# Gated linear attention between the projection chunks, and the output projection in two halves

## The reference

```python
sh1, sc1, gt1, sh2, sc2, gt2 = split(silu(c) @ w_ada + b_ada, 6)        # adaLN, w_ada 1024 x 6144
h = rms_norm(x, g_mix) * (1 + sc1) + sh1
gq, gk, gv, gg, glr, fq, fk, fv, ff = split(h @ w_in)                   # w_in 1024 x 3096
# GLA: 4 heads, key 64, value 128, blocks of 64 tokens (the sample has one block of 32)
log_a = log_sigmoid(glr @ w_gk2 + b_gk) / 16
o_gla = gla_chunked(gq, gk, gv, log_a, s0)     # scores in a block, states from block to block
o_gla = rms_norm(o_gla, g_gla) * silu(gg)
# FoX: 8 heads of 64, softmax(q k / 8 + cumulated log forget), the sample also over 512 cached rows
o_fox = rms_norm(fox_attention(fq, fk, fv, logf), g_fox)
x = x + gt1 * (concat(o_gla, o_fox) @ w_out)                            # the output projection
h = rms_norm(x, g_ffn) * (1 + sc2) + sh2
x = x + gt2 * (routed_experts(h, top 8 of 64) + shared_expert(h))       # gate, up: 1024 x 256, down: 256 x 1024
y = rms_norm(x, g_final)
```

## Time and profile before

| | |
|---|---|
| time, median of 3 runs | 796.29 us (795.01 to 797.1) |
| time of the profiled execution | 796.61 us |
| its span, first to last instruction | 794.9 us |
| mean granted TensorE clock | 0.951 |
| PE busy / VectorE / ScalarE / GpSimd | 743.5 / 358.7 / 227.0 / 49.6 us |
| moved by DMA | 254.51 MB, mean 320 GB/s |

### The profile page before, as it was taken

The page is one execution under the profiler, slowest core; times in us unless marked ns, Lnnn a source line. Parts: engine busy times, 40 slices in busy tenths (PEclk is TensorE's granted clock), DMA queues, the critical chain, the costliest instruction groups (busy, mean ns, idle before and its releaser), DMA issues.

```text
span 794.9 us, 15663 instructions
## 1 busy us (share of the span) xinstructions
PE 743.5 (94%) x4903; PEld 462.9 (58%) x4903; DVE 358.7 (45%) x955; ACT 227.0 (29%) x423; POOL 49.6 (6%) x217
## 2 busy tenths in 40 slices
PE   6599999779898898999999899999999999999994
PEld 3299997564688575544455455456444555445553
DVE  1464434643512573444444344344543445434456
ACT  2453335405511332222222122222222222222223
POOL 4000002320002100000000000000000000000033
PEclk9789998978789899999999999999999999999998
DMA  9965353927485423999999999999997899999951
GB/s 353 381 202 206 115 210 114 415 78 251 174 338 231 171 107 117 384 392 381 426 425 426 425 425 426 425 427 425 426 425 292 360 425 426 423 425 427 425 242 60
DMA packets 47183, 254.51 MB, mean 320 GB/s; under 512 B 9344, under 2 KB 9680, under 8 KB 19072
## 3 DMA queue, kind: packets, MB, share of 16 engines
q1 hardware_dynamic: 43616, 248.70, 77.1%
q10 hardware_dynamic: 2752, 3.32, 1.3%
q0 software_dynamic: 736, 1.52, 0.5%
HBM read 250.86 MB, written 2.67 MB: 319 GB/s over the span
## 4 chain that ended last, share of the span: by engine, by line
PE 85%; DMA 7%; DVE 5%; ACT 2%; issue 1%; SPq 0%; DVEq 0%; ACTq 0%
PE psum L1247 23%; PE psum L1283 11%; PE psum L941 9%; PE psum L1214 8%; DMA expert_w<-in_w_exp_up 5%; PE psum L1134 4%; PE psum L1228 4%; PE psum L1229 3%; PE psum L1221 3%; PE psum L1162 2%; PE psum L908 2%; DMA pair<-in_w_in 1%; PE psum L1152 1%; PE psum L1269 1%; PE psum L894 1%
## 5 line engine op out<-in xcount | busy, mean ns | idle before, releaser
L1247 PE MATMUL psum<-expert_w,xg 128*32 128x512 f32 (+1 forms) x1312 | 199.6, 596 | 4.9 <-DMA expert_w<-in_w_exp_up 3.4
L1247 PEld LDWEIGHTS psum<-expert_w,xg 128*32 128x32 f32 (+1 forms) x1312 | 60.5, 120 | 140.6 <-issue 139.0
L1713 DVE TENSOR_TENSOR acc<-psum,acc 128x288 f32<-128x288 f32 x224 | 97.0, 454 | 66.2 <-PE psum L1229 65.0
L1283 PE MATMUL psum<-expert_w,hidT 128*32 128x512 f32 (+1 forms) x656 | 102.1, 596 | 0.0
L1727 DVE TENSOR_TENSOR hid<-psum,silg 128x256 f32<-128x256 f32 x28 | 11.9, 425 | 143.9 <-ACT silg L717 143.9
L1214 PE MATMUL psum<-h2hl,sel 128*128 128x512 f32 x290 | 76.3, 393 | 0.5 <-ACT acc L699 0.5
L1228 PE MATMUL psum<-comb,yhi 128*128 128x288 f32 x224 | 74.3, 340 | 0.0
L1229 PE MATMUL psum<-comb,ylo 128*128 128x288 f32 x224 | 64.5, 295 | 0.0
L1283 PEld LDWEIGHTS psum<-expert_w,hidT 128*32 128x32 f32 (+1 forms) x656 | 28.1, 119 | 53.7 <-issue 53.7
L717 ACT ACTIVATE silg<-psum 128x256 f32<-128x256 f32 x28 | 10.7, 384 | 169.4 <-PE psum L1247 169.4
L1228 PEld LDWEIGHTS psum<-comb,yhi 128*128 128x128 f32 x224 | 42.5, 190 | 25.4 <-issue 23.1
(11 more groups left out here) (351 smaller groups left out, 931.5 us busy)
## 6 DMA issues: line engine op xcount, KB each, us to landing
expert_w<-in_w_exp_down SPq DMA_DIRECT2D x64, 1024.0 KB, 18.9
expert_w<-in_w_exp_gate SPq DMA_DIRECT2D x64, 1024.0 KB, 19.2
expert_w<-in_w_exp_up SPq DMA_DIRECT2D x64, 1024.0 KB, 19.8
ring<-in_w_ada SPq DMA_DIRECT2D x24, 1024.0 KB, 7.1
pair<-in_w_in SPq DMA_DIRECT2D x6, 2048.0 KB, 10.3
pair<-in_w_out SPq DMA_DIRECT2D x2, 2048.0 KB, 10.3
x_tok<-in_x_prompt SPq DMA_DIRECT2D x2, 512.0 KB, 4.4
cacheK<-in_cache_fox_k ACTq DMA_DIRECT2D x1, 1024.0 KB, 5.6
```

Of the source, the lines that this page charges most:

```text
L1247: last = mm(bank[3][at:at + w, :].rearrange("p (g n) -> p g n", g=2), xg[:, k, at:at + w], expert_w[:, q:q + 2, DE * k:DE * k + DE], start ...
L1283: last = mm(bank[4 + half][at:at + w, :], hidT[:, i, at:at + w], expert_w[:, slot_of(g, DOWN, x), o:o + 512], start=i == 0, stop=i == 1, t ...
L1713: dve.tensor_tensor(acc[:, k, :], bank[6 + k % 2][:, 0:N], acc[:, k, :], ALU.add).then_inc(s["acc_ok"], 1)
```

## The change

It moves work in the part ahead of the expert blocks, and leaves the code of the second norm, the router and the expert blocks as it is.

- **Start.** x's transposes, the sum of squares and `ada(0, 0..2)` are mixed on PE. Two of the four copies of `ada_rows(0)` go to VectorE, and three of the eight prompt parts of `hhi` (`HHI_DVE`). The first projection piece is loaded as two halves with counters of their own. Chunks 0 and 1 take their passes in turns (both high by high, both low by high, both high by low).
- **Projection.** Chunks rotate over banks 0 to 2 and no more over 0 to 3. Banks 4 to 7 hold what now stands between the chunks: narrow projections after chunk 3, gates after 5, transposes of the GLA values after 9, cumulated forget values after 11 and 13, `ada(1, k)` after 15, 17, 21 and 22, GLA scores after 18, state updates after 20, GLA outputs of the prompt after 22. VectorE and ScalarE take their parts in the same way, between a copy and the next `wlo` or `whi`.
- **Output gate.** silu(gg) is taken in one ScalarE instruction where it lies, features on partitions, and is multiplied in when the transposed output is copied out (`gated`). Its 12 transposes to tokens go. `o_tok` becomes `o_gla` and `o_fox`.
- **FoX.** The first two units start right after chunk 23; the GLA output of the sample, transposes of FoX values and keys, and those of the cached keys stand between their steps. The FoX key and value copies are shared by VectorE and ScalarE. The norm of o_gla and the transposes of it (`mixed_T(0..3)`) come in units 4 to 7, and `ada_T(2)` in the last.
- **Output projection.** `mix(k, range(4))` (the GLA half) for k = 0 to 3 before the FoX output is ready, then four transposes of `o_fox`, then the rest.

The core of the diff on PE:

```diff
         pe.wait_ge(s["sc_ok"], 1)
         for k in range(KC):
+            if k >= 4:
+                pe.wait_ge(s["xT_ok"], k - 3)
+            for i in range(3):
+                last = tr(bank[k % 4][:, T0[i]:T0[i] + TN[i]], x_tok[0:TN[i], i, k::KC], ident[0:TN[i], 0:TN[i]])
+            last.then_inc(s["xT_ps"], 1)
+            if k in (3, 6):
+                ada(0, k // 3 - 1, 5)
...
+        for c in range(24):
+            if c >= 3:
+                pe.wait_ge(s["z_act" if (c - 3) % 2 else "z_dve"], (c - 3) // 2 + 1)
+            if c >= 2:
+                z_pass(c, whi, hhi)
+                z_pass(c, wlo, hhi)
+            z_pass(c, whi, hlo).then_inc(s["z_ps"], 1)
+            if c == 3:
+                narrow()
+            if c == 5:
+                gates()
+            if c == 9:
+                gla_values()
+            if c == 11:
+                cumulate()
+            if c == 13:
+                cumulate_past()
+            if c in (15, 17):
+                ada(1, c - 15, 3)
+                ada(1, c - 14, 3)
+            if c == 18:
+                gla_scores()
+            if c == 20:
+                gla_updates()
...
+                gla_out(range(4))
...
+        for p in (2, 3):
+            pe.wait_ge(s["exp_ok"], LAST + p - 2)
+            mixed_T(p, o_gla, P * p)
         values(LAST)
...
+        pe.wait_ge(s["mT_dve"], 4)
+        for k in range(4):
+            if k == 3:
+                pe.wait_ge(s["ada_ok"], 3)
+            mix(k, range(4))
         pe.wait_ge(s["po_ok"], 3)
...
+        pe.wait_ge(s["fox_ok"], 3)
+        for p in range(4, KC):
+            mixed_T(p, o_fox, P * (p - 4))
```

and on ScalarE in the last units of FoX:

```diff
+            if u == 4:
+                act.wait_ge(s["ssq_act"], 12)
+                act.activation(rs5[:, :, 0:4], ssq5[:, :, 0:4], ACT.Sqrt, bias=epst[:, 0:1], scale=1.0 / GV).then_inc(s["rs_act"], 1)
             if u == 6:
+                ada_rows(2, 3)
                 act.wait_ge(s["po_ok"], 2)
```

More of the change, by code:

```diff
@@ L300, in layer, with hhi_of_act @@
     FIRST_KEY = (N + 1) * E
+    HHI_DVE = (1, 3, 5)
+    def hhi_of_act(k):
+        return len([x for x in range(k + 1) if x not in HHI_DVE])
     GATE, UP, DOWN = range(3)
@@ L631, in _ @@
[L631 to L634 removed]
+        ada_rows(1, 3)
         act.wait_ge(s["zeros"], 2)
@@ L923, in _ @@
         for k in range(KC):
+            if k >= 4:
[5 more added lines that the diff above has]
+                ada(0, k // 3 - 1, 5)
+        for k in range(KC):
+            pe.wait_ge(s["sq_ok"], k + 1)
+            last = mm(bank[6][:, 0:N], ones[:, :], sq[:, k, :], start=k == 0, stop=k == KC - 1)
+            if k == 3:
+                ada(0, 2, 5)
@@ L1011, in blocks, with cumulate_past @@
+        def cumulate_past():
+            pe.wait_ge(s["state_in"], 48)
+            pe.wait_ge(s["tok_dve"], 3)
+            for j in range(4):
+                for t in range(j, 4):
+                    last = mm(bank[4][0:FH, P * j:P * j + P], pastf[:, t, :], (lower if t == j else ones)[:, :],
+                              start=t == j, stop=t == 3)
+            last.then_inc(s["crow_ps"], 1)
+        def blocks(some):
+            for b in some:
                 i, pb, n = b // 2, 64 * (b % 2), BLK if b < 4 else NS_
@@ new lines, in z_pass @@
+        def z_pass(c, w, h):
+            g, q = c // 2, c % 2
+            pe.wait_ge(s["whi_ok" if w is whi else "wlo_ok"], g + 1)
+            for k in range(KC):
+                if c == 0 and h is hhi and w is whi:
+                    pe.wait_ge(s["hhi_act"], hhi_of_act(k))
+                    pe.wait_ge(s["hhi_dve"], k + 1)
+                if c == 0 and h is hlo:
+                    pe.wait_ge(s["hlo_ok"], k + 1)
+                last = mm(bank[c % 3][:, 0:N], w[g % 2][:, k, P * q:P * q + P], h[:, k, :],
+                          start=k == 0 and w is whi and h is hhi, stop=k == KC - 1 and h is hlo)
+            return last
@@ new lines, in mixed_T @@
+        def mixed_T(p, o, at):
+            for i in range(3):
+                last = tr(bank[MIX_BANK[p]][:, T0[i]:T0[i] + TN[i]], o[0:TN[i], i, at:at + P], ident[0:TN[i], 0:TN[i]])
+            last.then_inc(s["mT_ps"], 1)
+        scores(0)
+        scores(1)
+        pe.wait_ge(s["z_act"], 12)
+        pe.wait_ge(s["z_dve"], 12)
+        gla_out((4,))
+        for i in range(3):
+            if i == 2:
+                pe.wait_ge(s["go_ok"], 3)
+            tokens(i, FV0, TOK_BANK[i])
+        ada_T(1, 1)
@@ L1103, in _ @@
+        ada(2, 3, 3)
+        values(1)
+        scores(2)
+        for u in range(2, LAST + 1):
             if u < LAST:
                 scores(u + 1)
-            if u < 2:
-                ada(2, 2 * u, 3)
-                ada(2, 2 * u + 1, 3)
-            elif u < 6:
+            if u < 6:
                 ada(2, u + 2, 3)
+            if u == 6:
+                pe.wait_ge(s["gla_ok"], 3)
+                pe.wait_ge(s["po_ok"], 2)
+                mixed_T(0, o_gla, 0)
+            if u == LAST:
+                pe.wait_ge(s["mT_dve"], 1)
+                mixed_T(1, o_gla, P)
+                ada_T(2, 3)
```

718 lines of the change are left out of this document (402 added, 316 removed).

## The result

The changed kernel takes 784.12 us (median; 783.97 to 787.31) where the kernel before takes 796.69 in the same comparison. The ratio is 0.9852, 95% interval 0.9828 to 0.9877. It is faster, but by 12.6 us and not by the 29.7 that the sum gave, and it lies outside the range of 757 to 781. The profiled execution took 783.97 us (span 782.2, mean granted clock 0.965).

What follows compares the result with a forecast made beforehand. PE was taken as the bound: expert blocks unchanged, and a 254.7 us chain ahead with waits and half-rate work. Its terms summed to 225.0, 29.7 us sooner, so 796.6 became 767 us; range 757 to 781, its own 759 to 776.

Steps and rivals of the forecast that it cites:

- Chunks 2 to 23, 70.5: Projection chunks on PE: 70.5 us as before, with the three-bank rotation costing nothing.
- the rival by which it becomes the bound: Projection: VectorE's added steps make each `wlo` late, PE waits every 6.4 us, 800 us at 3.0 a pair; chance 0.04.
- Between the chunks, 32.4: Work inserted on PE between projection chunks, such as narrow products, transposes, `ada(1)` pieces and GLA steps: 32.4 us in sum.
- eight pieces of `ada(1)`, 0.885 each: 7.1: Term of the sum between the chunks: eight `ada(1)` pieces on PE at 5.31/6 = 0.885 us each, 7.1 us.
- Start, 4.5: Start to the end of chunk 1, 48.4 us before: 4.5 us sooner, bounds 2 and 6.
- there after 26.4 us ... nothing holds them back: Start: x and eight w_ada pieces landed after 26.4 us, pieces 6 and 7 issued early, 3.1 us sooner than 29.5.
- FoX, 18.3 + 23.8 + 3.0: Chunk 23 to unit 3 18.3 us, rest of FoX 22.8 plus 1.0 for ScalarE, and 3.0 for unplaced waits.
- Output projection, 33.1: Output projection: 31.0 us of mixing, plus 12 transposes 1.5 and the last copy 0.6, 33.1 in all.
- The clock falls at each insertion: Rival, between chunks: small matmuls and transposes lower the clock, 3.4 us at each of five places, 784 us; chance 0.13.
- The expert blocks don't start sooner: Rival, first expert block: loading its weights is not hidden and costs 10 us, 777 us; chance 0.05.
- Stalls beyond my allowance: Rival: stalls in FoX's first units or at the start, 785 to 797 us; chance 0.03.
- The rule against the row: Narrow products: skill has the clock fall only behind idle gaps, so 2.5 us would go, 764.4; the trace disagrees.

Runs made afterwards that it cites:

- the pieces later: Changed kernel with pieces 2 to 7 of ada(1) moved behind chunks 19, 22 and 23: 778.43 us, ratio 0.9718 to 0.9786 to the kernel before.
- the changed kernel again: The changed kernel, unedited, run once more as a reference on the chip of the second group of runs: 785.13 us.
- the squares first: Changed kernel with pieces ada(0, 0..2) put back behind the sums of squares on TensorE: 785.38 us.
- all repairs: Changed kernel with VectorE's copies ahead of xn, later ada(1) pieces, cacheV load behind chunk 21, and both engines' new order at FoX's end: 770.1 us.
- PE's order alone: Changed kernel with ada_T(2) and the first half's o_gla transposes behind unit 5's values on TensorE, VectorE's order kept: 778.4 us.
- the two with a new end of FoX: Changed kernel with TensorE's o_gla transposes behind unit 5's values and ada_T(2), with VectorE also reordered (778.74 us) or not (778.4 us).
- the pieces sooner: Changed kernel with ada(1) pieces 2 and 3 behind chunk 16, not 17, and 4 and 5 behind 20, not 21: 790.85 us.

## Why the prediction was wrong, step by step

*Chunks 2 to 23, 70.5.* Right: 1.23 us a pass at 1.00, no wait for a bank with three in rotation, and none for `wlo`. The lag of VectorE that "I count none" was none; the rival by which it becomes the bound fell.

*Between the chunks, 32.4.* This is the largest miss, 9.1 us (6.8 of waits, the rest half rate behind them), and the step that failed is "eight pieces of `ada(1)`, 0.885 each: 7.1". It priced the products and not their transfers. The rows of the changed kernel that show when a piece can come, its ScalarE, VectorE and SyncE's queue:

```profile
108.32 1.89 ACT L606 CAST whi<-pair 128x2048 fp32r<-128x2048 f32 x1
110.24 2.29 DVE L1517 TENSOR_TENSOR wlo<-pair,whi 128x2048 fp32r<-128x2048 f32 x1 [1.74 <-ACT whi L606]
112.57 33.46 SPq L501 DMA_DIRECT2D ring<-in_w_ada  x10
```

The slots of pieces 2 and 3 still hold weights of the projection. They come free when ScalarE and VectorE have made `whi` and `wlo` of the last of these; that can't begin before chunk 15 has given its `whi` buffer back (107.5), and it is done at 112.5. Then 1 MB is there 4.8 us later, at 117.35, and the next at 120.16. PE was there at 116.0. I followed the slots of the expert weights, and not these. With the pieces later the stage took 103.4: the other terms of the 32.4 (the narrow products with 2.5 behind them, transposes, cumulation, scores, updates, outputs) were right to 0.5 us in sum. Single ones were not: a piece is 0.92 us (1.83 for two), since the row of 5.31 us counts 45 products where six pieces have 48; and GLA's outputs, which the sum split by blocks, four to one, took 3.8 us for the prompt and not 5.1, and 2.7 for the sample and not 1.3.

*Start, 4.5.* It was 1.9 (2.8 in the changed kernel again). The step "there after 26.4 us ... nothing holds them back" failed twice. The last piece was through at 29.0, and by then it was no longer last: pieces on a half-rate PE (1.89 us where others take 1.04, though the clock's windows read 1.00 there) held up the squares, my lower bound's case, so the root ended at 26.5, not at 22.0 as in the run with the squares first, and VectorE had the reciprocal and `xn` (28.48 to 31.04) ahead of its copies. I took 1.2 for "copies halved" and did not look at what stands ahead of them on the second engine.

*FoX, 18.3 + 23.8 + 3.0.* It was 50.0. The allowance of 3.0 held 2.0 of waits (1.83 and 0.17). What the sum lacks is half rate: 164 to 171, behind the 32-row products of the sample, and 198 to 208, behind the wait of 1.83. Without both the stage took 42.7, under the 45.1.

*Output projection, 33.1.* It was 35.8: the first quarter ran at 0.82, 9.47 us, and 7.96 at full rate in the kernel with all repairs. That is 1.5 of 2.7. The other 1.2 is the size of terms: 12 transposes are 2.18 and not 1.5, and the mixing 31.4 and not 31.0 (7.96 + 23.48). Hiding the chain of o_fox beside the first quarter, which the change is built on, worked, and is worth 4.7 us.

*The rivals.* "The clock falls at each insertion" gave 784 and was wrong all the same. Of its five places none reads under 1.00; the 17 us that it added for five falls were missing at other places, for the reasons above. Its figure agreed by accident; the time alone would have passed it for the cause. "The expert blocks don't start sooner": their weights were issued at 220.2, 24 us ahead of the mixing's end, and PE never waited for them at the first block; 51.6 us lie between, 51.3 before. "Stalls beyond my allowance" (785 to 797) is nearest to what happened, at 0.03, and it named FoX and the start, not the projection.

*The rule against the row.* At the narrow products the window from 56 to 60 reads 1.00 and the next 0.70, PE busy 4.00 of 4.00 in both. So the fall without a gap came again, against what the Trainium skill, TensorE: Matmul & The Clock Gate, section "Why this matters for your kernels", has. For the end of FoX the same rule agrees in kind: with the gap gone, the clock stayed. But the gap there was one of 1.83 us, and the section speaks of longer ones.

## What to carry to other kernels

A product inserted into a stage without gaps is cheap only where its operand has landed: follow its ring slot back to the instruction that frees it, add the time to land, and place the product behind that. When a stage gets shorter, list every transfer that is asked for in it and put the one needed first ahead; the next wait is usually there. And a forecast that meets the number is shown right only by the rows of its mechanism: this one's rival met it within 0.2 us with no row behind it.

## What the runs showed of the hardware

A wait of 1.83 us is followed by some 14 us at 1.2 GHz (198 to 212), dense products included: the wait costs 1.8 us and what follows about 5 (7.3 + 1.5 of the two stages, less the 1.8 of the wait and the 1.8 further ahead). But it is no fixed price. In the changed kernel again, waits of 1.88 and 1.41 us between the chunks were followed by a piece at full rate, and in the kernel with PE's order alone, the same up to there, waits of 1.89 and 1.41 by one at half rate:

```profile
143.69 1.04 PE L947 MATMUL psum<-ring,scT 128*2 128x512 f32 x8 [1.41 <-DMA ring<-in_w_ada]
...
145.59 1.89 PE L947 MATMUL psum<-ring,scT 128*2 128x512 f32 x8 [1.41 <-DMA ring<-in_w_ada]
```

And GLA's 32-row products were followed by 0.50 in the changed kernel and by 1.00 in the two with a new end of FoX, which differ from it only behind that place (1.00 also with the squares first and with the pieces sooner). Which it will be can't be read from what PE did ahead of it in these runs.

With its queues full the core moved up to 430 GB/s (428 and 430 in the windows from 140 to 148, 426 to 415 in the four behind, at a DMA share of 1.01 or more), over the 364 GB/s of the earlier trace rows with which I worked out the start. The Trainium skill, DMA: Bandwidth & Descriptors, section "Measured (HBM→SBUF, 128 partitions, SWDGE, issued from GpSimd)", has 425 for 16 MB, issued from GpSimd; here most comes over SyncE's queue, and the trace agrees within 3%. A load of 1 MB asked for in such a stretch (cacheV with the late pieces) landed 23.8 us later; of the two asked for at 112.6 us, with nothing ahead of them, the first landed after 4.7 and the second after 7.2.
